# Fewer 512-column passes and more 256-column passes in the feed-forward tiles of an fp32 trunk, with h 128 bytes further on

## What is computed

```
x = x + 0.5 * _swiglu(_rms_norm(x, norm_ffn1[i]), ffn1_w_gate[i], ffn1_w_up[i], ffn1_w_down[i])
...
x = x + y        # y: the mixer's output
x = x + 0.5 * _swiglu(_rms_norm(x, norm_ffn2[i]), ffn2_w_gate[i], ffn2_w_up[i], ffn2_w_down[i])

def _swiglu(h, w_gate, w_up, w_down):
    return (jax.nn.silu(h @ w_gate) * (h @ w_up)) @ w_down
```

## Time and profile before

| | us |
|---|---|
| median of 3 runs | 1986.03 |
| lowest, highest | 1985.21, 1986.44 |
| span of the profiled execution | 1984.6 |
| TensorE busy in it | 1955.5 |
| VectorE busy in it | 1420.7 |
| ScalarE busy in it | 1044.4 |

### The profile page before, as it was taken

The page is one execution under the profiler, slowest core; times in us unless marked ns, Lnnn a source line. Parts: engine busy times, 40 slices in busy tenths (PEclk is TensorE's granted clock), DMA queues, the critical chain, the costliest instruction groups (busy, mean ns, idle before and its releaser), DMA issues.

```text
span 1984.6 us, 29082 instructions
## 1 busy us (share of the span) xinstructions
PE 1955.5 (99%) x12574; PEld 1717.6 (87%) x12574; DVE 1420.7 (72%) x1645; ACT 1044.4 (53%) x1250; POOL 101.6 (5%) x114
## 2 busy tenths in 40 slices
PE   7999999999999998999999999999999999999999
PEld 6888889888888896988888888788888888888887
DVE  7776678875787565877587658887758765778763
ACT  6554566554555344654465455575436544566542
POOL 3000001000200001100100000010000000001000
PEclk9999999999999998999999999999999999999999
DMA  7655434655665683665656553356566655435653
GB/s 238 194 183 182 149 128 154 192 188 189 192 191 180 201 249 83 191 191 182 200 191 192 177 184 128 107 176 191 183 196 190 191 183 180 148 128 171 191 189 107
DMA packets 336365, 350.14 MB, mean 176 GB/s; under 512 B 10077, under 2 KB 331886, under 8 KB 336238
## 3 DMA queue, kind: packets, MB, share of 16 engines
q1 hardware_dynamic: 331742, 343.58, 54.1%
q10 hardware_dynamic: 4496, 4.70, 1.2%
HBM read 346.04 MB, written 2.22 MB: 175 GB/s over the span
## 4 chain that ended last, share of the span: by engine, by line
PE 94%; DVE 3%; ACT 2%; issue 1%; POOL 1%; DMA 0%; ACTq 0%; DVEq 0%; POOLq 0%
PE banks L1443 49%; PE banks L1448 24%; PE banks L1434 5%; PE banks L1436 5%; PE banks L1435 5%; PE banks L1901 1%; PE banks L1660 1%; PE banks L1713 1%; ACT sb_w_high L470 1%; DVE sb_w_low L808 1%; PE banks L1680 1%; PE banks L1697 1%; ACT sb_scores L598 0%; PE banks L1818 0%; PE banks L1667 0%
## 5 line engine op out<-in xcount | busy, mean ns | idle before, releaser
L808 DVE TENSOR_TENSOR sb_w_low<-sb_raw,sb_w_high 128x2048 fp32r<-128x2048 f32 (+1 forms) x332 | 749.5, 2262 | 208.8 <-ACT sb_w_high L470 208.2
L1443 PE MATMUL banks<-sb_x_both,sb_w_high 128*128 128x512 f32 x2816 | 721.9, 393 | 1.9 <-ACT sb_w_high L470 1.9
L470 ACT ACTIVATE sb_w_high<-sb_raw 128x2048 fp32r<-128x2048 f32 (+1 forms) x332 | 618.5, 1867 | 122.2 <-DMA sb_raw<-in_ffn_w_down 109.0
L1443 PEld LDWEIGHTS banks<-sb_x_both,sb_w_high 128*128 128x128 f32 x2816 | 500.2, 189 | 82.2 <-ACT sb_w_high L470 2.3
L1448 PEld LDWEIGHTS banks<-sb_x_both,sb_w_low 128*128 128x128 f32 x2792 | 386.5, 188 | 35.2
L1448 PE MATMUL banks<-sb_x_both,sb_w_low 128*128 128x256 f32 x2792 | 394.6, 279 | 0.0
L1443 PE MATMUL banks<-sb_h_both,sb_w_high 128*128 128x512 f32 x1408 | 360.2, 395 | 0.0
L1443 PEld LDWEIGHTS banks<-sb_h_both,sb_w_high 128*128 128x128 f32 x1408 | 250.8, 188 | 45.3
L1448 PEld LDWEIGHTS banks<-sb_h_both,sb_w_low 128*128 128x128 f32 x1408 | 190.9, 188 | 16.9
L1448 PE MATMUL banks<-sb_h_both,sb_w_low 128*128 128x256 f32 x1408 | 194.4, 279 | 0.0
L488 ACT ACTIVATE sb_x_both<-sb_xT,sb_vec 128x256 fp32r<-128x256 f32 x96 | 43.3, 501 | 200.8 <-DVE sb_xT L841 176.1
(11 more groups left out here) (229 smaller groups left out, 1936.6 us busy)
## 6 DMA issues: line engine op xcount, KB each, us to landing
sb_raw<-in_ffn_w_gate SPq DMA_DIRECT2D x88, 1024.0 KB, 5.4
sb_raw<-in_ffn_w_up SPq DMA_DIRECT2D x88, 1024.0 KB, 5.3
sb_raw<-in_ffn_w_down SPq DMA_DIRECT2D x64, 1024.0 KB, 5.0
sb_raw<-in_ffn_w_down SPq DMA_DIRECT2D x32, 768.0 KB, 4.3
sb_raw<-in_fox_w_in SPq DMA_DIRECT2D x24, 1024.0 KB, 5.2
sb_raw<-in_conv_w_pw SPq DMA_DIRECT2D x12, 1024.0 KB, 5.4
sb_raw<-in_diff_w_in SPq DMA_DIRECT2D x12, 1024.0 KB, 5.0
sb_raw<-in_fox_w_out SPq DMA_DIRECT2D x8, 1024.0 KB, 4.8
```

Source lines behind the costliest of these rows:

```text
L470: act.activation(slot(w_high, b)[:, 0:width(b)], slot(raw, b)[:, 0:width(b)], ACT.Copy).then_inc(S["high_ready"], 1)
L808: dve.tensor_tensor(slot(w_low, b)[:, 0:width(b)], slot(raw, b)[:, 0:width(b)], slot(w_high, b)[:, 0:width(b)].bitcast(F32), ALU.subtract) ...
L1443: return pe.matmul(pair(bank[at][:, :]), high[:, n * P:(n + 1) * P], m_both, start=first, stop=last, skip_group_check=True)
```

## The change

The constant `WIDE = 3` and two helpers are new. `few_wide` replaces `both_parts` in `one_pair` and `down`: of a tile's k-tiles the first `wide` take w_high as one pass of 512 columns, as before; each other k-tile takes w_high as two passes of 256 columns (`on_part`), one with x_high into the left half and one with x_low into the right, each with its own load of the same weights. Then come all narrow low passes. `wide` is 3, except in the first two tiles after `sum_squares` (p = 1, `which` = 0), where it is 4 for n = 0 and 5 for n = 1. `first_pair` and `very_first_pair` keep `both_parts` and their own order. The gap `shift_h` grows from 200 to 232 elements, so `h_both` starts at 178,368, and everything behind it moves by 128 bytes too.

```diff
-        sb("shift_h", [P, 200])
+        sb("shift_h", [P, 232])
...
+            def on_part(at, n, high, m_part, half, first, last):
+
+                return pe.matmul(bank[at][:, half * SEQ:(half + 1) * SEQ], high[:, n * P:(n + 1) * P], m_part,
+                                 start=first, stop=last, skip_group_check=True)
+
+            def few_wide(at, n, high, low, m_both, ks, first, last, wide):
+
+                for k in ks[:wide]:
+                    on_both(at, n, high[:, k, :], m_both(k), first and k == ks[0], False)
+                for k in ks[wide:]:
+                    for half in range(2):
+                        on_part(at, n, high[:, k, :], m_both(k)[:, half, :], half,
+                                first and k == ks[0] and half == 0, False)
+                for k in ks[:-1]:
+                    on_high(at, n, low[:, k, :], m_both(k)[:, 0, :])
+                k = ks[-1]
+                return pe.matmul(bank[at][:, SEQ:2 * SEQ], low[:, k, n * P:(n + 1) * P], m_both(k)[:, 0, :],
+                                 start=False, stop=last, skip_group_check=True)
...
-                            ins = tile(which, p, n, range(KT))
+                            ins = tile(which, p, n, range(KT), WIDE if p > 1 or which else 4 + n)
...
-                        ins = both_parts(2 * (T % 2) + n, n, high, low, lambda k: h_both[:, :, first + k, :],
-                                         list(range(last - first)), c == 0, c == len(DOWN) - 1)
+                        ins = few_wide(2 * (T % 2) + n, n, high, low, lambda k: h_both[:, :, first + k, :],
+                                       list(range(last - first)), c == 0, c == len(DOWN) - 1, WIDE)
```

More of the change, by code:

```diff
@@ L35 @@
 RING = 5
+WIDE = 3
 FF_TILES = D_FF // P
@@ L1552, in ffn, with tile @@
                 b, f = starts[i], number(i)
-                def tile(which, p, n, ks):
+                def tile(which, p, n, ks, wide=None):
                     blk = b + 2 * p + which
                     high, low = (slot(t, blk).rearrange("p (k n) -> p k n", k=KT) for t in (w_high, w_low))
+                    if wide is not None:
+                        return few_wide(pair_banks(p) + 2 * which + n, n, high, low, lambda k: x_both[:, :, k, :],
+                                        list(ks), ks[0] == 0, ks[-1] == KT - 1, wide)
                     return both_parts(pair_banks(p) + 2 * which + n, n, high, low, lambda k: x_both[:, :, k, :],
```

## The result

| | before | after |
|---|---|---|
| median | 1985.62 us | 2005.08 us |
| lowest to highest, 4 runs each | 1984.10 to 1986.44 | 2004.05 to 2006.70 |
| span of the profiled execution | 1984.6 us | 2003.3 us |

The kernel before has one run more here than ahead of the prediction. The ratio is 1.0089, with an interval from 1.0077 to 1.0101. I had forecast 1968.4, and no more than 1980.

The account below looks back on a forecast made before the run. The prediction took the spacing of TensorE's passes to bound the FFNs. Gains of 8.7 (x tiles) and 10.2 (h tiles) less 0.3 and 1.0 gave 17.6 us, so 1968.4 us from 1986.0, range 1962 to 1980.

Parts of the forecast that it names:

- The bound: In the FFNs only the spacing of TensorE's passes counts; TensorE is busy 99% of the span and hardly waits.
- The two paces: A narrow pass (256 columns) takes 113.4 ns fast or 117.8 ns slow, and a run keeps its pace to its end.
- the rival's sum: For h tiles of down if all tiles run at the slow pace: 61.72 us per FFN; chance 0.08.
- every tile falls into the fast pace after at most two slow tiles and stays there: FFN tiles with three wide passes: fast stays fast, slow reaches fast; an x tile takes 2.728 us, gaining 8.7 us.
- The first two tiles: After sum_squares in one_pair: first tile slow with 4 wide passes, the second's five lead to fast; cost 0.3 us.
- Slow tiles left over: Up to two each behind first_pair in some FFNs, turn_vectors and final_turn; at most 1.3 us, taken as 1.0.
- The h tiles: In down, the address of h_both causes the extra 4 ns per wide pass; 61.31 falls to 60.03 us, gaining 10.2 us.
- The mixers: Their tensors move 128 bytes and start from other positions; 3 us either way allowed, taken as 0.
- The fixed prices: Rival: wide and narrow passes have fixed prices, the paces being mere noise; +2.0 us, 1988; chance 0.05.
- the fixed 2.5 ns per warm matmul: The skill's rule: each matmul costs its columns plus about 2.5 ns, so 2,408 added passes cost 6 us; 1992.
- the slow lock: Rival: in the FFNs all x and h tiles stay at the slow pace; 2005 us; chance 0.08.
- my cycle: Three positions, each wide pass stepping on by one; position 0 makes narrow runs fast, positions 1 and 2 slow.

Follow-up runs that it names:

- e1: The changed kernel, but in the seven later FFNs the second tile after sum_squares has 3 wide passes, not 5; 1973.74 us, ratio 0.9937 to the kernel before.
- e7: The changed kernel with 4 wide passes in every tile of one_pair and down; 1991.01 us, ratio 1.0019 to the kernel before.
- e3: The changed kernel with shift_h back at 200, so the split alone; 1999.68 us, ratio 1.0067 to the kernel before.
- e5: e1 with four wide passes in down's first tile behind turn_vectors (first FFN) and each final_turn (last FFN); 1969.48 us, ratio 0.9914 to the kernel before.
- e2: The kernel before with shift_h raised from 200 to 232 and nothing else; 1986.51 us, ratio 0.9997 to the kernel before.
- e8: The kernel before with x_both moved 128 bytes (shift_x 48, shift_h 168), h_both staying where it was; 1992.53 us, ratio 1.0027 to the kernel before.

## Why the prediction was wrong, point by point

**The bound** was right: nothing but the spacing of TensorE's passes moved in the FFNs, and no new wait appeared in them.

**The two paces** and the price of a tile at each were right. The changed kernel's h stretch is 61.71 us, and the rival's sum was 61.72; e1's is 60.00, and the forecast's 60.03.

**The step that failed** is the sentence that every tile falls into the fast pace after at most two slow tiles and stays there. It took the place that a string at the slow pace leaves behind to be independent of the string's length. All the strings that I had read on x had 8 or 2 passes, which act alike; the new tile has 18. I extended a law in the wide passes (rest by three, seen at 2 and 8) and never asked whether the narrow passes count in the same way, though the change more than doubles the length of their runs. e7 shows that they do.

**The first two tiles** failed as well. I carried over from the kernel before that the first tile would be slow, and I took its 16 narrow passes to leave a place two wide passes short of fast, so that the next tile's 5 would lead to fast. In the changed kernel `first_pair` ended behind a slow pair in all seven later FFNs, and the first tile came out fast; then 5 was the wrong number. I had listed that case, at a cost of two slow tiles. And where the first tile is slow as forecast, 5 is wrong too: e3 stays slow with it, and e1 shows that three wide passes lead back. With the loop it cost every tile of the FFN, 4.7 to 4.8 us each.

**Slow tiles left over** were to be at most two behind each fp32 interruption. With three wide passes they do not end by themselves: behind `turn_vectors` all 16 tiles of the first FFN's `down` that were left stayed slow in e1, and ten in the last FFN. e5 got 2.1 us back there, more than the 1.3 that I had as the most. It is the same failed step.

**The h tiles**: the address was the cause, as forecast (e2, e8). The gain of 10.2 us depended on the fast pace: with it e1's h stretch is 1.31 us below the 61.31 of before, and in the slow loop it is 0.40 above.

**The mixers**, taken as 0 within 3 us, cost some 3 us in the changed kernel. e2 shows that the gap alone costs 1.2 us in the first fox attention, where the changed kernel lost 1.0. Their `three_passes` are 2,880 in the profile, not 3,170; no term used that number.

**The fixed prices**, read from the rows, gave 1988. The runs disagree from both sides: e1 adds 2,422 passes to the kernel before and is 12 to 14 us faster, the changed kernel adds 2,408 and is 19 us slower. By the fixed 2.5 ns per warm matmul of the Trainium skill (TensorE: Matmul & The Clock Gate, "Wait — 56ns, not 53.3ns?") the estimate was 1992; these two runs do not fit it either.

**The rival that came true** is the slow lock. It named two ways. The first, that halves by turns move the position, is not needed: e1's fast tiles have the same halves by turns and stay fast. The second, that three wide passes close the cycle on a slow position, is what happened, though I had no reason to offer for it. That its price of 2005 met 2005.08 is partly luck: it put 19.3 us into eight FFNs, while seven locked and the FFNs lost 15.3, and the 3.5 us outside them made up the rest. I gave it 0.08 because I looked for something in the new passes that could break the cycle. The question that I should have asked is whether my cycle had a second fixed point.

## What to carry to other kernels

A deterministic pattern in the spacing of instructions is a state that is handed on, and a change of counts changes where it settles: write the state down with all that moves it, and search it for loops before trusting that it ends in the good one. A rule read from strings of 8 and 2 passes says nothing on strings of 18. And where one number at the entrance picks the loop, the entrance is the first thing to vary: here one tile's count of wide passes moved the time by some 31 us, more than the whole change.

## What the runs showed of the hardware that I had not expected

- The spacing of fp32r matmuls at the 2.4 GHz level depends on what went before: 256 columns take 113 or 118 ns, and a string keeps its pace to its end. In e1's seven later FFNs no tile behind the first left the fast pace up to the end of `down` (in the last FFN up to `final_turn`), while VectorE and ScalarE were busy for 90.08 and 63.12 of the 109.36 us of x tiles and DMA for 0.63, so it does not follow their moment-to-moment work.
- 128 bytes in the address of the streamed operand are worth 3 to 4 ns in a pass of 512 columns (1.86 against 1.84 or 1.83 us for eight), and they change which numbers of passes lead back to the fast pace. For 256 columns the two paces are the same at both addresses (0.91 us for eight in e8; 1.18 for ten in e3, and 1.14 for its fast strings, whose first pass takes some 5 ns more).
- An fp32 matmul in between can move the place: in e1 the first and third `final_turn` followed a string at the fast pace and left slow tiles with three wide passes behind them, the second followed a string at the slow pace and left tiles at the fast pace. One wide pass more in e5 mended those that had been slow. The pace before it alone does not fix the place behind it: in the changed kernel all three `final_turn` followed strings at the slow pace, and the tiles behind them were at the slow pace too. What else does is open.
- What the mechanism behind the places is, none of these runs tells.
